# A chunked linear recurrence on TensorE: the r and g projections of the next tile in one run at the head of the inverse half

## The reference

```
r, k, v, g = projections of h to 1024 channels each        (h: 512 tokens x 2048)
per direction: decays w, rates a, normalised keys, from k and two low-rank projections
state = state * w + (removal by the keys) + v k^T           (64 x 64 per head, token by token)
y = r . state, normalised per head, + bonus, * silu(g)
```

## Time and profile before

| | |
|---|---|
| median of 3 runs | 4041.18 us (4039.78 to 4047.8) |
| profiled execution: its own time | 4045.51 us |
| span of the profiled execution | 4043.7 us |
| mean granted TensorE clock | 0.969 |
| TensorE (PE) busy | 3862.1 us, 96% |
| VectorE (DVE) busy | 1404.3 us, 35% |
| ScalarE (ACT) busy | 677.4 us, 17% |
| GpSimd (POOL) busy | 193.8 us, 5% |
| eight tiles of the recurrence | from about 2590 to 3470 us of the span |
| first pp of tiles 1 to 7, at | 2712.5, 2827.6, 2942.7, 3056.4, 3171.5, 3285.1, 3389.9 us |

### The profile page before, as it was taken

The page is one execution under the profiler, slowest core; times in us unless marked ns, Lnnn a source line. Parts: engine busy times, 40 slices in busy tenths (PEclk is TensorE's granted clock), DMA queues, the critical chain, the costliest instruction groups (busy, mean ns, idle before and its releaser), DMA issues. The chain is left out here.

```text
span 4043.7 us, 65683 instructions
## 1 busy us (share of the span) xinstructions
PE 3862.1 (96%) x29122; PEld 2681.6 (66%) x29122; DVE 1404.3 (35%) x2850; ACT 677.4 (17%) x1597; POOL 193.8 (5%) x267
## 2 busy tenths in 40 slices
PE   5999999999999999999999999999999997899998
PEld 3446745554444676788658677666666666899998
DVE  1100143651012232212100531345444446655665
ACT  1100022420001122211100310222222222000000
POOL 0000000000000000000000000111122222000000
PEclk8999999999999999999999999999999997899999
DMA  8443322224333532455433234111111100345443
GB/s 343 172 151 140 125 84 105 101 88 166 125 142 108 183 145 76 157 211 197 145 137 126 83 116 146 63 45 45 35 34 45 45 23 33 115 161 181 159 171 121
DMA packets 73514, 490.00 MB, mean 121 GB/s; under 512 B 8448, under 2 KB 10496, under 8 KB 19472
## 3 DMA queue, kind: packets, MB, share of 16 engines
q1 hardware_dynamic: 70560, 462.45, 31.6%
q0 software_dynamic: 2672, 23.35, 1.5%
HBM read 481.57 MB, written 4.19 MB: 120 GB/s over the span
## 5 line engine op out<-in xcount | busy, mean ns | idle before, releaser
L1032 PE MATMUL ps<-h,w 128*128 128x512 f32 (+1 forms) x3456 | 1212.1, 498 | 21.7 <-ACT h L1658 14.2
L1032 PEld LDWEIGHTS ps<-h,w 128*128 128x128 f32 x3456 | 644.4, 193 | 433.4 <-issue 380.3
L1132 PE MATMUL ps<-h,w 128*128 128x256 f32 (+1 forms) x1024 | 413.3, 521 | 1.3 <-issue 1.3
L1032 PE MATMUL ps<-y,w 128*128 128x512 f32 (+1 forms) x1024 | 335.7, 488 | 0.2
L1032 PEld LDWEIGHTS ps<-y,w 128*128 128x128 f32 x1024 | 193.0, 190 | 133.2 <-issue 120.1
L1026 PE MATMUL ps<-w,h 128*128 128x256 f32 x1280 | 280.6, 380 | 0.0
L1026 PEld LDWEIGHTS ps<-w,h 128*128 128x128 f32 x1280 | 242.5, 190 | 39.3 <-issue 7.2
L2018 DVE TENSOR_TENSOR modc<-ps,bmod 128x4 f32<-128x4 f32 x72 | 11.4, 158 | 712.0 <-PE ps L985 711.9
L1132 PEld LDWEIGHTS ps<-h,w 128*128 128x128 f32 x1024 | 176.8, 194 | 91.7 <-issue 69.2
L1297 PEld LDWEIGHTS ps<-zone 64*64 64x64 f32 x4608 | 154.7, 140 | 52.4 <-issue 38.9
L1297 PE MATMUL ps<-zone 64*64 64x64 f32 x4608 | 176.0, 227 | 6.0 <-DVE zone L2303 5.9
(11 more groups left out here) (362 smaller groups left out, 4428.0 us busy)
## 6 DMA issues: line engine op xcount, KB each, us to landing
w<-in_wm SPq DMA_DIRECT2D x144, 1024.0 KB, 7.9
w<-in_we SPq DMA_DIRECT2D x52, 1024.0 KB, 5.2
w<-in_w SPq DMA_DIRECT2D x48, 1024.0 KB, 5.0
w<-in_wi SPq DMA_DIRECT2D x34, 1024.0 KB, 5.2
w<-in_wo SPq DMA_DIRECT2D x32, 1024.0 KB, 5.2
w<-in_wrw SPq DMA_DIRECT2D x32, 1024.0 KB, 5.0
w<-in_wmg SPq DMA_DIRECT2D x24, 1024.0 KB, 6.8
w<-in_wbr SPq DMA_DIRECT2D x48, 512.0 KB, 4.2
```

What stands on the lines that cost most here:

```text
L1032: last = mm(pass_psum(s, q), rows[:, n * P:(n + 1) * P], src[k], start=(k == 0), stop=(k == s.kt - 1))
L1132: last = mm(ps[:, m, 0:T - NC * n], halves.rows(k)[:, m * P:(m + 1) * P], h[:, k, NC * n:T], start=(k == 0), stop=(k == KT - 1))
```

## The change

TensorE no longer issues the r and g passes of tile it+1 in pieces. All 32 products come in one run at the head of `rw_invert(it)`, ahead of the waits for `s_ff` and `s_yev`. The pieces of two behind `rw_transpose(it, 0)` and the pieces of one or two in every step of the loop are gone. Nothing else is touched: no other engine's program, no wait and no number of instructions.

```diff
             def rw_invert(it, passes=iter(())):
 
-                def fill(n):
-
-                    for _ in range(n):
-                        next(passes, None)
-
                 def beside(n):
...
-                fill(2)
+                for _ in passes:
+                    pass
                 pe.wait_ge(s_ff, it + 1)
                 if it >= 1:
                     pe.wait_ge(s_yev, it)
...
                 rw_transpose(it, 0)
-                fill(2)
                 for n in range(21):
...
                         beside(n)
-                        fill(2 if n % 2 else 1)
...
                         last.then_inc(s_dt, 1)
-                for _ in passes:
-                    pass
```

## The result

The changed kernel takes 4021.79 us, the median of four runs (4016.7 to 4026.89), beside 4044.49 us before (4039.78 to 4047.89): a ratio of 0.9944, 95% interval 0.9929 to 0.9959. That is 23 us or 0.56% faster, where 4035.5 us with a range of 4026 to 4054 had been forecast. The profiled execution took 4026.89 us with a span of 4025.1 us, 18.6 us under the span of before.

What follows compares the result with a forecast made beforehand. TensorE, busy 96% of the span, was taken as the bound. Per tile 13.0 - 13.1 - 1.9 = -2.0 us, over all tiles -11.3; with +5.5 for the tail's clock, -5.8: 4035.5 us, range 4026 to 4054.

Steps and rivals of the forecast that it cites:

- The joints: In the loop, changing from 64x64 to 128x128 products and back costs 0.34 us per fill, at most 6.5 us per tile.
- The lost cover at the head: At each tile's head, 30 more products add 13.0 us; the gap ahead of the first pp becomes 4.37 us.
- From the first pp to update 12: This stretch of the loop falls by 13.1 us, from 43.84 in tile 2 to tile 7's 30.76 us.
- From update 12 to line 1342: At the loop's end VectorE becomes late and TensorE waits; the stretch falls by 1.9 us, from 12.9 to 11.0.
- The clock in the tail: Low clock expected in most tails, from update 12 on: 0.85 us each, 6.5 times, +5.5 us.
- The spells at the head: Low clock behind the gap ahead of the first pp, mean 0.52 over 10.5 us in tile 2; no term in the sum.
- rival three: Low spell behind the first pp is cut short without its three fill products, 1.4 us per tile: 4020 us, chance 0.05.
- the sum without the clock: All tiles' changes at head, loop and tail before any low clock in the tail: -11.3 us.
- Rival one: The clock holds in the tail: -11.3 us, 4030 us, with 4024 to 4033 for errors in the walk; chance 0.33.
- Rival two: Clock falls in the tail and stays low some 10.5 us into the recurrence: 3.3 us per tile, +12, 4053 us; chance 0.20.

Runs made afterwards that it cites:

- fewer joints: Kernel before the change with the same products in the loop in ten fills instead of 19, nothing moved to the head; 4022.99 us, ratio 0.9941.

## Why the prediction was wrong

- **The joints** (0.34 us per fill): right, and shown by themselves with half as many.
- **The lost cover at the head** (+13.0 us, gap 4.37 us): measured from the start of the first product at the head to line 1183, 0.95 us before and 13.91 us after, +12.96; the gap 4.25.
- **From the first pp to update 12** (30.76 us, read from tile 7): 29.93 us in tile 2 (2833.06 to 2862.99). The term is 0.8 us too long, and that is the clock: of tile 7's spell 8.6 us lie behind its first pp, of that of tile 2 in the changed kernel 6.8.
- **From update 12 to line 1342** (11.0 us): 11.03. The waits on the way are 1.38, 0.70 and 0.37 us, where 1.6, 0.9 and 0.6 had been walked out.
- **The clock in the tail** (+5.5 us): the step that failed. It was "So I expect a spell of low clock in most tails", with the recurrence of tile 7 as the nearest row. There was none. The rows that were nearer in what matters were those with the lengths of the single waits: 1.4 us in the tail, 3.4 us at the head, 5.9 us in tile 7. In the tails no wait of up to 1.54 us brought a spell and every one of 4.8 us or more did. At the heads, gaps of 2.3 to 2.5 us brought one in six tiles of seven, and longer ones in every tile of every profile but one (tile 2 with fewer joints). The busy share of a stretch didn't tell the two cases apart: TensorE is busy 2.62 and 2.68 of 4 us in the two windows of the tail and keeps its clock, and 2.06 and 1.72 of 3 us in tile 7's recurrence, where it falls. What brings it down there, with no wait over 0.74 us ahead of it in that recurrence, stays open. The rule of the Trainium skill, "TensorE: Matmul & The Clock Gate", section "Why this matters for your kernels", which puts the fall of the clock down to long idle gaps, agrees with the tails of these runs (no spell at waits of up to 1.54 us, one at each wait of 4.8 us or more) and was the better guide; with tile 7's recurrence it does not.
- **The spells at the head** (taken as unchanged): rival three, given 0.05, was half right. The tiles' time is 19.4 us shorter (798.6 to 779.2). The low clock behind the first pps fell by 63.0 - 46.3 = 16.7 us, which at half speed is up to 8.3 us of them. That products in the spell cost this much is shown by the three put back, nothing else changed: 30.3 us more of low clock behind the first pps (76.6), so up to 15.1 us, and two joints more in seven tiles, 4.8 us at the full clock, make 19.9, where the tiles' time grew by 18.6. By the medians it is 23 us; what makes the other 4 isn't shown. Why a product lengthens a spell isn't shown either.
- So the sum without the clock was right, as far as this count goes: -11.3 us beside -19.4 + 8.3 = -11.1. The clock had been taken at +5.5 us and gave -8.3. That is 13.8 of the 16.9 us by which the effect was too small (-5.8 forecast, -22.7 by the medians); the rest is what the medians gain outside the tiles' time, and noise. The start of the forecast, 4041.18 us, was by chance 3.3 us below the median of four, 4044.49. That hid 3.3 us of the error, so that 4035.5 misses by only 13.7.
- **Rival one** (the clock holds, 4030 us, chance 0.33) had the tail right; the measured time lies below its 4024 to 4033 because of the spells at the head.
- **Rival two** (slower) had its place right, for a wait of 5 us and not for the change's 1.4 us, but not its price: the spells last 3.4 or 6.8 us and not 10.5, and cost 1 to 1.5 us per tile and not 3.3. Both rows quoted for and against it were read too short. Tile 6 did recover after 3.4 us, but 3.4 us later, at 3357.6, its clock fell again for 27.3 us; tile 7's did recover, 27.3 us after its fall. The window of the kernel before, tile 6:

```profile
3357.50:3384.50 27.00, 21.52 (x379) 18.23 (x380) 16.66 (x37) 5.74 (x16) 0.97 (x2) 0.50 0.01 2
```

## What to carry to other kernels

Products that fill latency beside a chain of another tile shape cost a joint each time: put them in few, long fills, and put those where the engine waits anyway, first of all into the longest gap, since that one also costs the clock behind it. Here the same 32 products took the kernel from 4045 to 4022 us in one run at the head, and to 3968 us when ten of them filled the gap and three the waits of the tail. And keep such work out of the time that runs at low clock: three products there cost all that the rest had gained.

## What was not expected of the hardware

- Behind the heads' gaps the clock's spells come in lengths of 3.4, 6.8, 10.2 or 13.7 us, whatever the kernel, and the same tile can have 6.8 us in one profile and 10.2 in the next. How long one lasts depends on what is issued in it: with three 128x256 products between the 64x64 ones, in the otherwise changed kernel, it was 10.2 or 13.7 us in each of seven tiles, without them 3.4 to 10.2. Why more work makes it longer is open.
- In the recurrences of the last two tiles the clock falls in every profile, in most for 27.3 or 30.7 us at a time; with no wait over 0.74 us ahead of it in that of tile 7, and behind waits of 1.83 us in that of tile 6. What decides there is open.
- VectorE and GpSimd slow each other: one and the same operation took 0.74 and 1.52 us, and a copy of 7 elements per partition on GpSimd 0.19 and 1.18 us, in each of tiles 0 to 6.
